# Softmax heads of 128 values: the product of the first keys' values with the probabilities in three rounded products

## Chip, cores and metric

The kernel runs on one core of one Trainium2 chip. The metric is the device time of one execution in microseconds (us). Before the change it is 1800.07 us, the median of three runs (1799.96 to 1800.71).

## The reference, cut to what matters

Four layers are applied to 256 tokens of width 2048. Each layer multiplies the normalised input with a wide weight matrix, mixes the tokens in several kinds of heads, and multiplies the result with an output matrix. All of it is in fp32. The change touches one kind of head alone, the softmax heads with 128 values:

```python
# layer 0, 8 heads (chunk_rel_attention); BAND and rel_bias give which keys count, and a bias
p = jax.nn.softmax(sc, axis=-1)
o = jnp.einsum('bhnqk,bnkhd->bnqhd', p, vb)
# layer 2, 8 heads (_dilated_mixture): causal, keys weighted by how many dilated windows hold them
# layer 3, 16 heads (_moba_attention): one block of 256 keys, so plain causal attention
s_own = jnp.where(kpos[None, :] <= qpos[:, None], s_own, -jnp.inf)
p = jax.nn.softmax(s_own, axis=-1)
return jnp.einsum('bhij,bhjd->bhid', p, vo)
```

That makes 32 such heads. Layer 2 has eight more score maps, which belong to four differential heads of 256 values; layer 1 has no softmax. The change does not touch those.

## The kernel before, in words

**The weights set the rhythm.** All weight matrices together are cut into 633 pieces of 512 KB. For each piece p, SyncE loads RAW; ScalarE rounds it to WH (the high part, type fp32r, in `split`, L1222); VectorE subtracts the two and gets WL (the low part, `split`, L1654); TensorE multiplies WH and WL with the activations, which are kept in high and low parts as well (`products`, L838 to L853). Three rounded products, high by high, low by high and high by low, stand there for one fp32 product. ScalarE and VectorE split piece p+5 in the iteration in which TensorE multiplies piece p. ScalarE may not split piece p+5 before TensorE has finished piece p-1, because there are six WH buffers.

**Everything else hangs on the pieces.** A plan, made at build time, says which small steps follow which piece. Each engine runs through the pieces in order, in one instruction stream without reordering. For piece p ScalarE and VectorE first do the `split` of piece p+5; GpSimd has no split. Then, on all three, come the steps planned half a slot before, then `evacuate` if a weight matrix block (a job) ends with piece p, then the steps planned for p. TensorE does the products and then its planned steps. In the heads plan, TensorE's order within one slot is pv, pT, scores, qkT.

**A softmax head of 128 values** (`heads_plan`) goes through these steps, one round of four pieces apart:

- `scores`: TensorE multiplies queries and keys (L960, L961) into a PSUM bank; VectorE scales and masks (L1857) and takes the row maxima (L1862, L1864); ScalarE takes the exponent with the row sum (L1382, L1384); VectorE takes the reciprocal (L1884, step `rsum`); ScalarE multiplies (L1389, L1390, step `normal`, half a slot later).
- `pT`: TensorE turns the probabilities (three 128x128 transposes, L976); ScalarE copies them out of PSUM into the slot `pt_slot` in SC (L1365).
- `pv`: TensorE multiplies the values with the turned probabilities: the first 128 keys with all 256 queries (L998, fp32) and the last 128 keys with the last 128 queries (L999, fp32). VectorE (L1901), or ScalarE for heads 24 to 31 (L1429), takes the result out.

**Where the heads run.** The 8 heads of layer 0 run beside the pieces of its z and o gates, the 8 of layer 2 and heads 32 to 39 of layer 3 beside the z blocks and the first output pieces. Heads 24 to 31, the first half of layer 3, are placed elsewhere: beside the pieces of the queries and keys of the second half (jobs q1 and k1 of layer 3, four blocks each). `pT` and `pv` of these eight stand one slot later (`late` in `heads_plan`), the two steps of one head four pieces apart. With each of the eight blocks a rope job ends: VectorE adds the two halves of the accumulator and multiplies with sine and cosine (`evacuate`, kind rope, L1721, L1727, L1729), and then GpSimd adds the two parts (`evacuate` of GpSimd, L2210). On VectorE, that rope job stands in the iteration of the block's last piece, after the split of that iteration. The iterations in which these blocks end are those one slot after `pT`.

**GpSimd's queue** holds, in order of the pieces: the rope additions (L2210), the loads of the bias of layer 0's heads with a wait for their landing (L2214, L2216), products with gates (L2193, L2238), and some additions at the end of a layer.

Of the kernel before, what the change touches and what calls it, by code (L numbers as in the profile page):

```python
# [8 lines left out]
F32 = mybir.dt.float32  # L9
F32R = mybir.dt.float32r  # L10
ALU = mybir.AluOpType
ACT = mybir.ActivationFunctionType
# [155 lines left out]
def program(nc, I, out):  # L168
    ctx = ExitStack()
    with ctx:  # L170
        def sb(name, cols, dt=F32, where=ctx):
            return where.enter_context(nc.sbuf_tensor(name, [128, cols], dt))

        def sem(name):
            return ctx.enter_context(nc.semaphore(name))
# [10 lines left out]
        SEL, _ = sb("SEL", 768, F32R), sb("Y_REST", 2 * D - 768)  # L186
# [6 lines left out]
        WH = [sb(f"WH{i}", 1024, F32R) for i in range(NHL)]  # L193
        SC = sb("SC", 4096)
        C = sb("C", CW)
        ZC = sb("ZC", 1024)
        S5 = sb("S5", 2048)
        S6 = sb("S6", 2048)
        S0 = sb("S0", 2048)
# [24 lines left out]
        def tok(i):  # L224
            return two(S[i][:, :])
# [43 lines left out]

        def qk_slot(g):  # L270
            return SC[:, 512 * (g % 3):512 * (g % 3) + 512]

        def sc_slot(g):
            return SC[:, 1536 + 384 * (g % 3):1920 + 384 * (g % 3)]

        def pt_slot(g):
            return SC[:, 2688 + 384 * (g % 3):3072 + 384 * (g % 3)]
# [101 lines left out]
        def at_A(*key):  # L379
            return A_AT[J_OF[key]]  # L380
# [11 lines left out]
        def head_of(a):  # L392
            return (0, 0, a) if a < 8 else (2 + (a - 8) // 16, (a - 8) // 8 % 2, a % 8)
# [14 lines left out]

        TURN = list(accumulate(0 if g >= 4 and first_of_pair(g - 4) else 1 for g in range(44)))

        def masked(a):

            return 2 * a + 2 if a < 8 else a + 9
# [9 lines left out]
        def put(slot, step, item=0, wants=0):  # L423
            plan.setdefault(slot, []).append((step, item, wants))
# [23 lines left out]
        def heads_plan(first, slot, every):  # L448
            for r in range(11):
                for i, step in ((3, "pv"), (2, "pT"), (1, "scores"), (0, "qkT")):  # L450
                    if step == "qkT" and first >= 8:
                        continue
                    h = r - i + (first >= 8)
                    if 0 <= h < 8:
                        late = 1 if first == 24 and step[0] == "p" else 0
                        put(slot + every * r + late, step, first + h + (4 if step[0] == "p" else 0), 1)
                        if step == "scores":
                            put(slot + every * r, "rsum", first + h)
                            put(slot + every * r + 0.5, "normal", first + h)
# [155 lines left out]
        def around(p):  # L615
# [13 lines left out]
        s_hi, s_lo, s_mm, s_evA, s_evD = (sem(n) for n in ("s_hi", "s_lo", "s_mm", "s_evA", "s_evD"))  # L629
# [8 lines left out]
        s_qkT, s_qk, s_sc, s_msk, s_mx, s_rc, s_mix, s_mixA, s_ex, s_pt, s_pts, s_pv, s_ho = (  # L638
            sem(n) for n in ("s_qkT", "s_qk", "s_sc", "s_msk", "s_mx", "s_rc", "s_mix", "s_mixA", "s_ex", "s_pt", "s_pts", "s_pv", "s_ho"))
# [5 lines left out]
            sem(n) for n in ("s_one", "s_sel", "s_dgz", "s_dgh", "s_dgl", "s_dgt", "s_mdh", "s_mdl", "s_mdt", "s_zc"))  # L645
        s_dg, s_pa, s_pe, s_pk, s_pc, s_pm, s_zero, s_am, s_tri, s_la = (
            sem(n) for n in ("s_dg", "s_pa", "s_pe", "s_pk", "s_pc", "s_pm", "s_zero", "s_am", "s_tri", "s_la"))
        s_neg = sem("s_neg")
        s_lx, s_lc, s_ly, s_ld, s_so, s_sd, s_sa, s_or, s_on, s_gd1 = (
            sem(n) for n in ("s_lx", "s_lc", "s_ly", "s_ld", "s_so", "s_sd", "s_sa", "s_or", "s_on", "s_gd1"))  # L650
        s_lg, s_li, s_lxg, s_le, s_lq, s_ls, s_zs, s_zg, s_zh, s_zl = (
# [127 lines left out]
        def tensor(e):  # L779
# [200 lines left out]
            def values_of(g):  # L980

                if g < 4:
                    return [tok(2)[:, t, 256 * g:256 * g + 256] for t in range(2)], 256, (0, "vb", (0, 1, 2, 2)[g])
                layer, n, h = head_of(g - 4)
                if is_diff(g - 4):
                    c = slice(256 * (h // 2), 256 * (h // 2) + 256)
                    return [tok(2)[:, t, c] for t in range(2)], 256, (2, "v0", h // 4)
                c = slice(128 * h, 128 * h + 128)
                return [tok(3 * n + 2 if layer else 5)[:, t, c] for t in range(2)], 128, (layer, f"v{n}" if layer else "va", h // 4)

            def pv(g, b):
                v, dv, job = values_of(g)
                e.wait_ge(s_pts, TURN[g])
                e.wait_ge(s_evA, at_A(*job))
                e.wait_ge(s_evD, at_D(*job))
                o, p = bank(b), pt_slot(g)
                if dv == 128:
                    e.matmul(o[:, 0:256], v[0], p[:, 0:256], start=True, stop=False, skip_group_check=True)  # L998
                    e.matmul(o[:, 128:256], v[1], p[:, 256:384], start=False, stop=True, skip_group_check=True).then_inc(s_pv)  # L999
                    read_out[b] = finished(g - 4)  # L1000
                    return
                e.matmul(o[:, 0:dv], p[:, 0:128], v[0], start=True, stop=True)
                e.matmul(o[:, dv:2 * dv], p[:, 128:256], v[0], start=True, stop=False)
                e.matmul(o[:, dv:2 * dv], p[:, 256:384], v[1], start=False, stop=True).then_inc(s_pv)
                read_out[b] = (s_mo, 2 * g + 2) if g < 4 else finished(g - 4)
# [195 lines left out]
        def scalar(e):  # L1201
# [161 lines left out]
            def pT(g, b):  # L1363
                e.wait_ge(s_pt, TURN[g])
                e.activation(pt_slot(g), PM[b][:, 0:384], ACT.Copy).then_inc(s_pts)  # L1365

            def norm_qk(_, b):
                for j in range(2):
                    e.wait_ge(s_qsq, 16 * j + 16)
                    e.activation(ssA[j], ssA[j], ACT.Sqrt, bias=vec("eps"), scale=1.0 / 128).then_inc(s_nq)  # L1370
# [202 lines left out]
            def gate_c(item, _):  # L1573
                b, i = item
                z = ZC[:, 512 * i:512 * i + 512]
                e.wait_ge(s_evD, at_D(1, "zc", b) - 1 + i)
# [12 lines left out]
            def subln(part, _):  # L1589
                if part == 0:  # L1590
# [1 line left out]
                    e.activation(ss, ss, ACT.Sqrt, bias=vec("eps"), scale=1.0 / 256).then_inc(s_sln)  # L1592

            steps = {"seed": seed, "warm": warm, "xt": xt, "squares": squares, "root": root, "rms_a": rms_a, "gates1": gates1, "selectors": selectors, "decay_cols": decay_cols,
                     "decay_rows": decay_rows, "cols": columns_step, "rows": rows, "decay": decay, "pT": pT,
                     "norm_qk": norm_qk, "qkT": qkT, "scores": scores, "normal": normal, "silu_z": silu_z, "yT": yT, "mix1": mix1, "pv": pv, "ty": ty, "copied": copied, "silu": silu, "decays1": decays1,
                     "decays2": decays2, "norm_sq": norm_sq, "norm_sum": norm_sum, "turn_v": turn_v, "delta_a": delta_a, "tri": tri, "small_x": small_x,
                     "spread_t": spread_t, "level_x": level_x, "level_y": level_y,
# [20 lines left out]
            for t in range(2):  # L1619
                c = slice(1536, 2048)  # L1620
# [558 lines left out]
        def gpsimd(e):  # L2179
# [50 lines left out]
            def scores(a, b):  # L2230
                if a < 6:
                    e.wait_ge(s_msk, 2 * a + 2)
                    load_bias(a + 2)

            def gate_z(i, _):
                e.wait_ge(s_zT, ZT.index(J_OF[3, "zg", i]) + 1)
                e.wait_ge(*finished(24 + 2 * i + 1))
                e.tensor_tensor(y_pair(4 + i), y_pair(4 + i), z_of(J_OF[3, "zg", i]), ALU.mult).then_inc(s_gz)  # L2238
# [41 lines left out]
            def gained(b, _):  # L2280
# [3 lines left out]
                for t in range(2):  # L2284
                    e.wait_ge(s_evD, at_D(3, "out", b) - 1 + t)
                    e.tensor_tensor(Y3[:, t, c], X3[:, t, c], S0[:, c], ALU.mult).then_inc(s_gn)

            steps = {"norm_qk": norm_qk, "scale_k": scale_k, "scores": scores, "gate_z": gate_z, "cols": columns_step, "tri": tri, "gate_w": gate_w,
                     "gate_lru": gate_lru, "gate_c": gate_c, "load_mask": load_mask, "load_gain": load_gain, "gained": gained}

            def go(todo):
# [84 lines left out]
```

## Time and profile before

| what | value |
|---|---|
| median of 3 runs | 1800.07 us |
| the profiled execution | 1799.72 us |
| its span, first to last instruction | 1797.8 us |
| TensorE, products busy | 1788.5 us, 99% |
| TensorE, weight loads busy | 1622.1 us, 90% |
| VectorE busy | 1243.6 us, 69% |
| ScalarE busy | 1037.5 us, 58% |
| GpSimd busy | 154.5 us, 9% |
| mean granted TensorE clock | 0.999 |

How to read it: PE is TensorE's products, PEld its weight loads, DVE is VectorE, ACT is ScalarE, POOL is GpSimd. A product that streams many columns overlaps the end of the one before it, so TensorE's spacing is read from start to start and not from the duration of one. An fp32 product appears as two instructions of each kind in the trace. Where rows join several instructions ("x2"), the time is from the first start to the last end. The time outside the span is 1.9 us.

### The profile page before, as it was taken

To read this page: it belongs to the slowest core of one execution; us is meant where nothing else is said; L and a number is where in the kernel's file an instruction comes from. 1 tells how busy PE (TensorE), PEld (TensorE's weight loads), DVE (VectorE), ACT (ScalarE), POOL (GpSimd) and SP (SyncE) were. 2 spreads that over 40 slices of the span, in tenths; PEclk is the share of its full clock that TensorE was granted. 3 is DMA by queue.
4 is the path that set the end of the run, shared out by engine and by line. 5 is a ranking of instruction groups with operands and counts; after the bars stand their busy time and mean duration, and the time that the engine had idled before them with its cause. 6 is when DMAs were issued, how large, how long until landed. Compare 5 with 4: busy or idle time off the path is not lost.

```text
span 1797.8 us, 27226 instructions
## 1 busy us (share of the span) xinstructions
PE 1788.5 (99%) x10842; PEld 1622.1 (90%) x10842; DVE 1243.6 (69%) x1711; ACT 1037.5 (58%) x1638; POOL 154.5 (9%) x116
## 2 busy tenths in 40 slices
PE   9999999999999999999999999999999999999998
PEld 8999889888899999998889999898888999989987
DVE  6665656665666897687658888776565888767764
ACT  7435546774557765875554345576454444457853
POOL 0000000110011111100001211000000111100110
PEclk9999999999999999999999999999999999999999
DMA  9557555555555555445566655555555655555564
GB/s 370 200 171 225 182 182 190 181 175 195 190 189 167 171 171 175 154 165 169 194 207 202 199 188 176 193 180 172 190 193 196 201 199 181 174 192 183 168 220 140
DMA packets 95901, 340.30 MB, mean 189 GB/s; under 512 B 10800, under 2 KB 11184, under 8 KB 95648
## 3 DMA queue, kind: packets, MB, share of 16 engines
q1 hardware_dynamic: 94400, 334.44, 55.9%
q0 software_dynamic: 944, 3.61, 0.6%
q8 instruction: 86, 1.41, 0.3%
q10 hardware_dynamic: 432, 0.53, 0.1%
q14 instruction: 39, 0.32, 0.1%
HBM read 336.44 MB, written 2.10 MB: 188 GB/s over the span
## 4 chain that ended last, share of the span: by engine, by line
PE 99%; DMA 0%; DVE 0%; issue 0%; ACT 0%; DVEq 0%
PE ACC L838 15%; PE ACC L840 15%; PE ACC L839 15%; PE ACC L846 12%; PE ACC L843 12%; PE ACC L845 6%; PE ACC L844 6%; PE ACC L851 2%; PE ACC L852 2%; PE ACC L853 2%; PE PM L961 1%; PE PM L998 1%; PE PM L976 1%; PE PM L890 1%; PE PM L960 0%; PE PM L999 0%
## 5 line engine op out<-in xcount | busy, mean ns | idle before, releaser
L1654 DVE TENSOR_TENSOR WL<-RAW,WH 128x1024 fp32r<-128x1024 f32 (+2 forms) x631 | 793.4, 1272 | 421.8 <-ACT WH L1222 420.3
L1222 ACT ACTIVATE WH<-RAW 128x1024 fp32r<-128x1024 f32 (+2 forms) x632 | 646.9, 1038 | 382.5 <-PE ACC L840 190.2
L843 PE MATMUL ACC<-XHL,WH 128*128 128x512 f32 x1024 | 395.6, 386 | 0.0
L846 PE MATMUL ACC<-XHL,WH 128*128 128x512 f32 x1024 | 391.2, 382 | 0.0
L838 PE MATMUL ACC<-WH,XHL 128*128 128x512 f32 (+1 forms) x788 | 296.5, 376 | 0.0
L840 PE MATMUL ACC<-WH,XHL 128*128 128x512 f32 (+1 forms) x788 | 291.9, 370 | 0.0
L839 PE MATMUL ACC<-WL,XHL 128*128 128x512 f32 (+1 forms) x788 | 291.9, 370 | 0.0
L845 PE MATMUL ACC<-XHL,WL 128*128 128x256 f32 x1024 | 281.6, 275 | 0.0
L844 PE MATMUL ACC<-XHL,WL 128*128 128x256 f32 x1024 | 279.1, 273 | 0.0
L845 PEld LDWEIGHTS ACC<-XHL,WL 128*128 128x128 f32 x1024 | 193.5, 189 | 27.4
L844 PEld LDWEIGHTS ACC<-XHL,WL 128*128 128x128 f32 x1024 | 193.6, 189 | 26.5
L843 PEld LDWEIGHTS ACC<-XHL,WH 128*128 128x128 f32 x1024 | 196.5, 192 | 1.3
L846 PEld LDWEIGHTS ACC<-XHL,WH 128*128 128x128 f32 x1024 | 196.6, 192 | 0.0
L840 PEld LDWEIGHTS ACC<-WH,XHL 128*128 128x128 f32 x788 | 148.9, 189 | 18.5
L838 PEld LDWEIGHTS ACC<-WH,XHL 128*128 128x128 f32 x788 | 149.0, 189 | 18.0 <-DVE WL L1654 0.2
L839 PEld LDWEIGHTS ACC<-WL,XHL 128*128 128x128 f32 x788 | 149.0, 189 | 17.8
L2210 POOL TENSOR_TENSOR S<-S 128x512 f32<-128x512 f32 x32 | 66.5, 2078 | 479.3 <-DVE S L1729 479.3
L851 PE MATMUL ACC<-XHL,WH 128*128 128x256 f32 x384 | 106.7, 278 | 0.0
L852 PE MATMUL ACC<-XHL,WH 128*128 128x256 f32 x384 | 105.6, 275 | 0.6 <-issue 0.6
L853 PE MATMUL ACC<-XHL,WL 128*128 128x256 f32 x384 | 105.6, 275 | 0.0
L838 PE MATMUL ACC<-WH,YHB 128*128 128x512 f32 x256 | 98.1, 383 | 0.0
L839 PE MATMUL ACC<-WL,YHB 128*128 128x512 f32 x256 | 97.0, 379 | 0.0
(406 smaller groups left out, 2344.0 us busy)
## 6 DMA issues: line engine op xcount, KB each, us to landing
RAW<-in_w SPq DMA_DIRECT2D x607, 512.0 KB, 3.3
RAW<-in_wv SPq DMA_DIRECT2D x24, 344.0 KB, 3.2
X<-in_x SPq DMA_DIRECT2D x4, 512.0 KB, 11.9
Y<-in_xT SPq DMA_DIRECT2D x3, 512.0 KB, 10.6
out<-Y SPq DMA_DIRECT2D x6, 256.0 KB, 3.6
S<-in_bias POOLq DMA_DIRECT2D x8, 128.0 KB, 2.3
S<-in_od_gate_w POOLq DMA_DIRECT2D x1, 1024.0 KB, 7.1
S<-in_final_norm POOLq DMA_DIRECT2D x1, 1024.0 KB, 6.3
```

The costliest lines, as they stand in the source:

```text
L838: e.matmul(o, th, wh, start=f, stop=False, skip_group_check=seeded)
L839: e.matmul(o, th, wl, start=False, stop=False, skip_group_check=seeded)
L840: m = e.matmul(o, tl, wh, start=False, stop=l, skip_group_check=seeded)
L843: e.matmul(acc[0], wh0, pairs, start=f, stop=False, skip_group_check=True)
L844: e.matmul(acc[0][:, 0:256], wl0, pairs[:, 0], start=False, stop=l, skip_group_check=True)
L845: e.matmul(acc[1][:, 0:256], wl1, pairs[:, 0], start=f, stop=False, skip_group_check=True)
L846: m = e.matmul(acc[1], wh1, pairs, start=False, stop=l, skip_group_check=True)
L851: e.matmul(o, wh, pairs[:, 0], start=f and g % 2 == 0, stop=False, skip_group_check=True)
L852: e.matmul(o, wh, pairs[:, 1], start=False, stop=False, skip_group_check=True)
L853: m = e.matmul(o, wl, pairs[:, 0], start=False, stop=l, skip_group_check=True)
L1222: e.activation(hi, src, ACT.Copy).then_inc(s_hi)
L1654: e.tensor_tensor(lo, src, hi.bitcast(F32), ALU.subtract).then_inc(s_lo)
```

## The change

A tile PVH of 1024 columns of type fp32r is laid over ZC, which layer 1 alone uses. For each of the 32 heads a step `pv_split` is planned one slot after `pT`. In it ScalarE rounds the head's values of the first 128 keys (128x128) and the first 256 columns of the turned probabilities (128x256) into PVH, and GpSimd subtracts and leaves the low parts in PVH. PVH has one set of halves, so ScalarE waits for the `pv` of the head before. In `pv`, TensorE waits for GpSimd's second subtraction and then does three fp32r products of 256 columns in place of the fp32 product of L998. The product of the last 128 keys (L999) stays in fp32. GpSimd's `pv_split` stands in its `steps`, which run after `evacuate` of the same iteration.

```diff
-        ZC = sb("ZC", 1024)
+        with ExitStack() as first:
+            ZC = sb("ZC", 1024, F32, first)
+        PVH = sb("PVH", 1024, F32R)
...
+        def pv_halves():
+
+            return [PVH[:, x:y] for x, y in ((0, 256), (256, 512), (512, 640), (640, 768))]
...
+        def values_at(g):
+
+            layer, n, h = head_of(g - 4)
+            c = slice(128 * h, 128 * h + 128)
+            return [tok(3 * n + 2 if layer else 5)[:, t, c] for t in range(2)], (layer, f"v{n}" if layer else "va", h // 4)
+
+        def split_heads(g):
+
+            return g - 4 if g < 12 else g - 12
...
                         put(slot + every * r + late, step, first + h + (4 if step[0] == "p" else 0), 1)
+                        if step == "pT":
+                            put(slot + every * r + late + 1, "pv_split", first + h + 4)
...
# TensorE, pv
                 if dv == 128:
-                    e.matmul(o[:, 0:256], v[0], p[:, 0:256], start=True, stop=False, skip_group_check=True)
+                    ph, pl, vh, vl = pv_halves()
+                    e.wait_ge(s_pvl, 2 * split_heads(g) + 2)
+                    e.matmul(o[:, 0:256], vh, ph, start=True, stop=False, skip_group_check=True)
+                    e.matmul(o[:, 0:256], vl, ph, start=False, stop=False, skip_group_check=True)
+                    e.matmul(o[:, 0:256], vh, pl, start=False, stop=False, skip_group_check=True)
                     e.matmul(o[:, 128:256], v[1], p[:, 256:384], start=False, stop=True, skip_group_check=True).then_inc(s_pv)
...
# ScalarE
+            def pv_split(g, _):
+                v, job = values_at(g)
+                ph, _, vh, _ = pv_halves()
+                if g > 4:
+                    e.wait_ge(s_pv, TURN[g] - 1)
+                e.wait_ge(s_evA, at_A(*job))
+                e.activation(vh, v[0], ACT.Copy).then_inc(s_pvh)
+                e.wait_ge(s_pts, TURN[g])
+                e.activation(ph, pt_slot(g)[:, 0:256], ACT.Copy).then_inc(s_pvh)
...
# GpSimd
+            def pv_split(g, _):
+                v, _ = values_at(g)
+                ph, pl, vh, vl = pv_halves()
+                e.wait_ge(s_pvh, 2 * split_heads(g) + 1)
+                e.tensor_tensor(vl, v[0], vh.bitcast(F32), ALU.subtract).then_inc(s_pvl)
+                e.wait_ge(s_pvh, 2 * split_heads(g) + 2)
+                e.tensor_tensor(pl, pt_slot(g)[:, 0:256], ph.bitcast(F32), ALU.subtract).then_inc(s_pvl)
```

## Rows read from the trace of the kernel before

**Rows 1.** The page's chain that ended last, by engine, as shares of the span.

```profile
PE 99%; DMA 0%; DVE 0%; issue 0%; ACT 0%; DVEq 0%
```

**Rows 2.** TensorE's longest wait of all: total us, times, longest us.

```profile
PE PM L882 <- DVE S L1732: 1.5, 1, 1.5
```

**Rows 3.** Line L998: duration min/median/max in ns, first and last start, form.

```profile
L998 PE MATMUL PM<-SC,S x64: 379/379/379, 327.9 to 1723.0; 128*128 128x256 f32 x64
```

**Rows 4.** Timeline of TensorE, first `pv` of layer 3: start, duration, instruction.

```profile
1503.68 0.59 PE L998 MATMUL PM<-SC,S 128*128 128x256 f32 x2
1504.11 0.39 PE L999 MATMUL PM<-SC,S 128*128 128x128 f32 x2
```

**Rows 5.** Timeline of TensorE, fp32r products of 256 columns: two of them.

```profile
545.49 0.28 PE L851 MATMUL ACC<-XHL,WH 128*128 128x256 f32 x1
...
548.84 0.28 PE L851 MATMUL ACC<-XHL,WH 128*128 128x256 f32 x1
```

**Rows 6.** Groups of ScalarE's instructions by form: busy us, mean ns, idle before.

```profile
L1244 ACT ACTIVATE S<-S 128x128 f32<-128x128 f32 x32 | 9.9, 310 | 11.3 <-DVE S L1696 10.2
L1222 ACT ACTIVATE WH<-RAW 128x256 fp32r<-128x256 f32 x1 | 0.4, 401 | 0.0
```

**Rows 7.** Lines of GpSimd: duration min/median/max in ns, first and last start, form.

```profile
L2262 POOL TENSOR_TENSOR S<-S x8: 727/733/1490, 739.5 to 749.7; 128x256 f32<-128x256 f32 x8
L2210 POOL TENSOR_TENSOR S<-S x32: 1275/2192/2197, 955.6 to 1580.3; 128x512 f32<-128x512 f32 x32
```

**Rows 8.** Timeline of DVE, ACT and POOL, one round of layer 3's first heads.

```profile
1501.49 3.44 DVE L1654 TENSOR_TENSOR WL<-RAW,WH 128x1024 fp32r<-128x1024 f32 x2
1501.66 2.19 POOL L2210 TENSOR_TENSOR S<-S 128x512 f32<-128x512 f32 x1 [10.65 <-DVE S L1729]
1504.86 0.54 DVE L1857 SCALAR_TENSOR_TENSOR SC<-PM,C 128x384 f32<-128x384 f32 x1
1505.83 0.40 ACT L1382 ACTIVATE SC<-SC,SM 128x128 f32<-128x128 f32 x1 [6.72 <-DVE SM L1862]
...
1508.36 0.36 ACT L1429 ACTIVATE Y<-PM 128x256 f32<-128x256 f32 x1
...
1510.07 1.22 DVE L1654 TENSOR_TENSOR WL<-RAW,WH 128x1024 fp32r<-128x1024 f32 x1 [1.05 <-ACT WH L1222]
...
1514.61 3.42 DVE L1654 TENSOR_TENSOR WL<-RAW,WH 128x1024 fp32r<-128x1024 f32 x2
```

**Rows 9.** Timeline, last rope job of layer 3 and the `pv` due then.

```profile
1575.64 0.59 PE L998 MATMUL PM<-SC,S 128*128 128x256 f32 x2
...
1580.16 1.22 DVE L1654 TENSOR_TENSOR WL<-RAW,WH 128x1024 fp32r<-128x1024 f32 x1
...
1580.32 2.19 POOL L2210 TENSOR_TENSOR S<-S 128x512 f32<-128x512 f32 x1 [10.91 <-DVE S L1729]
1581.30 2.30 DVE L1654 TENSOR_TENSOR WL<-RAW,WH 128x1024 fp32r<-128x1024 f32 x1
```

**Rows 10.** Timeline, layer 1: a GpSimd product between two splits of VectorE.

```profile
648.49 1.95 DVE L1654 TENSOR_TENSOR WL<-RAW,WH 128x1024 fp32r<-128x1024 f32 x1
649.32 2.26 POOL L2205 TENSOR_TENSOR S<-S,C 128x512 f32<-128x512 f32 x1
...
650.37 2.29 DVE L1654 TENSOR_TENSOR WL<-RAW,WH 128x1024 fp32r<-128x1024 f32 x1
```

**Rows 11.** Timeline, layer 1: a GpSimd product beside VectorE's reads of PSUM.

```profile
600.98 1.28 POOL L2205 TENSOR_TENSOR S<-S,C 128x512 f32<-128x512 f32 x1
...
601.23 0.28 DVE L1998 TENSOR_TENSOR SC<-PM,C 128x128 f32<-128x128 f32 x1
```

**Rows 12.** Timeline of ACT and PE, a round of layer 0's heads.

```profile
333.62 0.50 ACT L1390 ACTIVATE SC<-SC,SM 128x256 f32<-128x256 f32 x1
...
340.32 0.59 PE L998 MATMUL PM<-SC,S 128*128 128x256 f32 x2
```

**Rows 13.** Busy us of each engine, granted clock and DMA, heads 24 to 31.

```profile
1478.00:1590.00 112.00, 112.00 (x663) 102.22 (x662) 89.97 (x103) 55.13 (x102) 18.05 (x9) 1.00 0.54 179
```

More of the change, by code:

```diff
@@ L647, in program @@
             sem(n) for n in ("s_dg", "s_pa", "s_pe", "s_pk", "s_pc", "s_pm", "s_zero", "s_am", "s_tri", "s_la"))
-        s_neg = sem("s_neg")
+        s_neg, s_pvh, s_pvl = sem("s_neg"), sem("s_pvh"), sem("s_pvl")
         s_lx, s_lc, s_ly, s_ld, s_so, s_sd, s_sa, s_or, s_on, s_gd1 = (
@@ L987, in values_of @@
                     return [tok(2)[:, t, c] for t in range(2)], 256, (2, "v0", h // 4)
-                c = slice(128 * h, 128 * h + 128)
-                return [tok(3 * n + 2 if layer else 5)[:, t, c] for t in range(2)], 128, (layer, f"v{n}" if layer else "va", h // 4)
+                v, job = values_at(g)
+                return v, 128, job
             def pv(g, b):
@@ L1365, in pT @@
                 e.activation(pt_slot(g), PM[b][:, 0:384], ACT.Copy).then_inc(s_pts)
+            def pv_split(g, _):
+                v, job = values_at(g)
+                ph, _, vh, _ = pv_halves()
[5 more added lines that the diff above has]
+                e.activation(ph, pt_slot(g)[:, 0:256], ACT.Copy).then_inc(s_pvh)
             def norm_qk(_, b):
@@ L1594, in scalar @@
             steps = {"seed": seed, "warm": warm, "xt": xt, "squares": squares, "root": root, "rms_a": rms_a, "gates1": gates1, "selectors": selectors, "decay_cols": decay_cols,
-                     "decay_rows": decay_rows, "cols": columns_step, "rows": rows, "decay": decay, "pT": pT,
+                     "decay_rows": decay_rows, "cols": columns_step, "rows": rows, "decay": decay, "pT": pT, "pv_split": pv_split,
                      "norm_qk": norm_qk, "qkT": qkT, "scores": scores, "normal": normal, "silu_z": silu_z, "yT": yT, "mix1": mix1, "pv": pv, "ty": ty, "copied": copied, "silu": silu, "decays1": decays1,
@@ L2286, in gained @@
                     e.tensor_tensor(Y3[:, t, c], X3[:, t, c], S0[:, c], ALU.mult).then_inc(s_gn)
-            steps = {"norm_qk": norm_qk, "scale_k": scale_k, "scores": scores, "gate_z": gate_z, "cols": columns_step, "tri": tri, "gate_w": gate_w,
+            steps = {"norm_qk": norm_qk, "scale_k": scale_k, "scores": scores, "pv_split": pv_split, "gate_z": gate_z, "cols": columns_step, "tri": tri, "gate_w": gate_w,
                      "gate_lru": gate_lru, "gate_c": gate_c, "load_mask": load_mask, "load_gain": load_gain, "gained": gained}
```

## The prediction

> **What bounds the kernel now.** I read the chain of waits first: TensorE holds 99% of it [rows 1]. The list of TensorE's waits then says whether anything holds it up: the longest wait is 1.5 us and comes at the start [rows 2]. So TensorE is the bound from end to end; work on the other engines costs nothing until TensorE waits for it, and every us that TensorE saves or loses moves the end. A sum over TensorE's instructions is therefore half of the question. The other half is whether the new operands are there when TensorE comes to them, and for that I read the timelines round by round. Averages mislead here: in the stretch of heads 24 to 31 VectorE is busy 90.0 of 112 us, ScalarE 55.1 and GpSimd 18.1 [rows 13], and yet, below, that is the place that decides.
>
> **TensorE's own part.** The fp32 product (two instructions a head, 64 in all [rows 3], so 32 heads) runs from 1503.68 to the start of its successor at 1504.11 [rows 4]: 0.43 us. The new products are of the form of the layer-1 ones, fp32r, 256 columns, a weight load for each. Between the two rows shown there are 30 of them from start to start [rows 5]: 3.35 / 30 = 0.112 us, three make 0.335. A head saves 0.095, 32 heads 3.04 us. Bounds: the rows round to 0.01 us, which is 0.3 us over 32 heads, so 2.7 to 3.4; a stall of a weight load between the two types is in no row, and the fp32 pair that follows shows none after fp32r products before.
>
> The Trainium skill, "FP8 and Floating Point Precision", section TensorE Precision Notes, counts four passes for a true fp32 product. By that rule a pass is 0.43 / 4 = 0.107, three products save one pass, and 32 heads would save 3.4 us; the rows give 0.112 for a product with its own weight load, and the sum keeps those.
>
> **ScalarE's part.** The nearest rows are 0.31 us for 128x128 and 0.40 for 128x256 [rows 6], 0.71 a head and 23 us in all. In heads 24 to 31 it comes behind the splits that ScalarE does before it stands idle for 6.72 us, waiting for VectorE's maxima [rows 8]; it is hidden there. Without that cover it would delay the exponent by 0.71 a round. Its new wait, for the `pv` of the head before, is met already, since its copy of `pT` waited for a later TensorE step. If it weren't, the splits of the weights would queue behind it.
>
> **GpSimd's part.** The nearest rows are 0.73 for 128x256 undisturbed and 1.28 for 128x512 [rows 7]; on the line through both, 128x128 is 0.45. So 1.18 us a head, 38 us in all, on an engine that is nearly idle. What counts is its place in the queue. In heads 24 to 31 the subtractions stand behind the rope addition of the same iteration, and the addition waits for VectorE's rope job. TensorE needs the result three pieces later.
>
> **VectorE is late there already, and nobody waited for it.** VectorE's round, from the end of one rope job to that of the next, is read from the pair of splits that follows each: 1501.49 [rows 8] to 1580.16 [rows 9] in six rounds, 13.11 us each. TensorE's round, from `pv` to `pv`, is 1503.68 [rows 4] to 1575.64 [rows 9] in six: 11.99. VectorE's loop has its own chain (maxima, exponent, ScalarE's split and copies, where it waits 1.05 us [rows 8], then the split, the rope job), so it falls behind by about 1.1 us a round and uses up the five pieces of lead that the weights have. It just suffices: TensorE never waits in this stage. The new wait changes which lead counts. `pv` at 1575.64 will need a subtraction that stands behind a rope job ended at 1580.16: even with subtractions that cost nothing, TensorE would stand there for 4.5 us.
>
> **The sum, on the old clock.** The first of these heads: the rope addition ends at 1501.66 + 2.19 = 1503.85 [rows 8]. The addition takes 2.19 where it takes 1.28 alone [rows 7], because it waits for VectorE's split to end, and the second split takes 2.30 instead of 1.22 because it then waits for the addition [rows 9]: the two take turns, and whoever waits goes next. In layer 1 a GpSimd product behind another one lets the split of 648.49 go first, ends at 651.58, 1.14 after that split's end at 650.44 (0.14 less than alone), and the next split in turn ends at 652.66, 1.08 after it [rows 10]. So the first subtraction waits until the second split ends, 1501.49 + 3.44 = 1504.93, takes 0.45 - 0.14 = 0.31, and the second 0.73 behind it, until 1505.97. Both are free of VectorE, which is at the masking then [rows 8], an instruction that reads PSUM; such ones run at 0.28 beside a GpSimd product that takes its normal 1.28 [rows 11]. TensorE comes at 1503.68: it waits 2.3 us. Five more heads add VectorE's lag, 1.1 each. At the seventh and last with a rope job in front, VectorE goes on with splits, without masking between: the second split ends at 1583.60 [rows 9], first subtraction 1583.91, third split 1584.99, second subtraction 0.73 - 0.14 later, 1585.58. TensorE would come at 1575.64, less the six savings of 0.095 since the first of these heads: 1575.07. All waits of the stage together are 10.5 us. The eighth head has no rope job in front and is in time.
>
> I looked for what the waits set off. Behind the waiting `pv` queue on TensorE its own `pT` and all further pieces; ScalarE's copies of both wait for them. ScalarE comes to those copies at 1508.36 [rows 8], and the `pv` released at 1505.97 is through by 1506.5, so VectorE's loop isn't slowed. Weights are ahead of TensorE all the more. The other 24 heads: in layer 0 ScalarE's normalising ends at 334.12 and TensorE's next `pv` starts at 340.32 [rows 12]; 0.71 on ScalarE and 1.18 on GpSimd, with a turn for one split (1.08), end by 337.1. The rope additions lie between 955.6 and 1580.3 [rows 7], so none is in the queue of heads 32 to 39; layer 2's softmax heads have theirs behind them as well.
>
> Net: 10.5 - 3.0 = 7.5 us longer. On the profiled execution (1799.72: its span of 1797.8 and 1.9 around it) that is 1807.2; the median of the runs is 0.35 above that execution, so I predict **1807.6**.
>
> **Bounds of the waits.** Least: no turn is lost to splits in the last round, 1582.51 + 0.45 + 0.73 = 1583.7, waits of 8.6, time 1805.7. Most: the first subtraction loses a turn to a third split as well (1.08 more) and ScalarE's 0.71 shows once, 12.3, time 1809.4. I take the middle, nearest to the turns of rows 10.
>
> The Trainium skill, "SBUF — State Buffer", section Who interferes with whom, says that a VectorE instruction with two inputs in SBUF and a GpSimd instruction that reads SBUF exclude each other, for a whole instruction. The trace agrees (2.19 and 2.30 against 1.28 and 1.22 above). By it the last subtraction ends at 1585.6; were the two merely to share, it would be the 1583.7 of the lower bound.
>
> **Rivals.**
> *Covered after all* (0.12). The subtractions arrive in time and only TensorE's saving shows: 1800.07 - 3.0 = 1797.0. For it: GpSimd is busy 9% and the `pv` is three pieces behind. Against: the order in the queue, and 1580.16 against 1575.64. It decides from the point where GpSimd is through by 1503.68 in the first round.
> *GpSimd holds up VectorE* (0.08). Each subtraction takes a turn from VectorE's loop, and its rounds get longer, not only TensorE's. For it: the 2.30 split. Against: the masking reads PSUM. At 0.3 in each of six rounds 1.8 more, 1809.4; at both subtractions' whole turns, 0.9, 5.4 more, 1813.0.
> *TensorE's clock* (0.04). The mean granted clock is 1.00 in this stage, the upper level, with no idle time before [rows 13]. Waits of 2 to 3 us are new, and if the grant falls to 1.2 GHz after the last of them, a piece of 2.6 us (a quarter of TensorE's round, less its head steps) takes 2.6 more: 1810.2. In the rounds before it, the next wait would swallow that.
> The Trainium skill, "TensorE: Matmul & The Clock Gate", section Why this matters for your kernels, warns of such gaps in a stream of products; no row here shows a fall after one.
>
> **How the numbers follow.** Forecast 0.76, own range 1805.7 to 1809.4. From 1804.0 to 1811.0 I leave out the first rival and the far end of the second and third. A measurement of this kernel tells 0.2%, 3.6 us, from no change: slower means above 1803.7. The forecast and the last two rivals lie there, 0.88. The covered case is 0.17% faster, so 0.08 of its 0.12 goes to no change and 0.04 to faster.
>
> **What would show it.** In the changed profile, TensorE's waits should list `pv` waiting for GpSimd's PVH seven times, about 2.3, five times 1.1, and 2.9 at the last, 10 to 11 us in all, between 1500 and 1590, and none for the other 25 heads. The three products should start 0.11 apart. GpSimd's subtractions should directly follow the rope addition in those seven, VectorE's rounds there should stay at 13.1, and ScalarE should be busy some 23 us more. I am wrong if TensorE waits elsewhere, if it doesn't wait, or if VectorE's round changes.

## The result, and the profile after

The changed kernel takes 1807.93 us (median of 6 runs, 1807.16 to 1811.07); the kernel before took 1800.43 us (6 runs, 1799.96 to 1801.66, three of them those of the table before). The ratio is 1.0044, with an interval of 1.0031 to 1.0057: slower by 0.44%, clear of noise. The forecast was 1807.6, its own range 1805.7 to 1809.4.

The profiled execution took 1811.07 us, at the upper end of its runs. A second profiled execution of the same kernel took 1807.63, and sums are made against that one. Of the 3.4 us between the two, 1.7 arose at the start and 1.7 behind the last wait, both with products at half the rate (told at the end). One execution in the experiments, of the reordered kernel without heads 29 and 30, fell in a slow state at 6973.81 us and is left out of its median and ratio.

The page after, busy time by engine: against the page before, GpSimd has 51.2 us more and ScalarE 15.9; none of it is on the path but the subtractions of the seven heads below.

```profile
PE 1790.9 (99%) x10874; PEld 1623.7 (90%) x10874; DVE 1244.5 (69%) x1711; ACT 1053.4 (58%) x1702; POOL 205.7 (11%) x180
```

TensorE's waits after (us in total, times, longest), which answer to [rows 2]. The first row is new: the first of the three products waits for GpSimd's second subtraction seven times. The second row is the 1.5 us at the start that was there before.

```profile
PE PM L1018 <- POOL PVH L2273: 8.9, 7, 2.6
PE PM L900 <- DVE S L1764: 1.5, 1, 1.5
```

Timeline after, the first of the heads of layer 3 and the last with a rope job in front (answering to [rows 4, 8 and 9]). The rope addition L2242 and the two subtractions L2271, L2273 follow each other on GpSimd; the first product L1018 starts when the second subtraction is through, and TensorE is idle for 2.23 and 2.56 us before it. In the last rows the second product starts 0.19 behind the first, and the pair behind the three 0.43.

```profile
1501.68 3.44 DVE L1686 TENSOR_TENSOR WL<-RAW,WH 128x1024 fp32r<-128x1024 f32 x2
1501.85 2.19 POOL L2242 TENSOR_TENSOR S<-S 128x512 f32<-128x512 f32 x1 [10.65 <-DVE S L1761]
1504.00 1.43 POOL L2271 TENSOR_TENSOR PVH<-S,PVH 128x128 fp32r<-128x128 f32 x1
1505.40 0.72 POOL L2273 TENSOR_TENSOR PVH<-SC,PVH 128x256 fp32r<-128x256 f32 x1
1506.26 0.36 PE L1018 MATMUL PM<-PVH 128*128 128x256 f32 x1 [2.23 <-POOL PVH L2273]
...
1580.32 4.83 DVE L1686 TENSOR_TENSOR WL<-RAW,WH 128x1024 fp32r<-128x1024 f32 x3
1580.48 2.19 POOL L2242 TENSOR_TENSOR S<-S 128x512 f32<-128x512 f32 x1 [8.84 <-DVE S L1761]
1582.63 1.43 POOL L2271 TENSOR_TENSOR PVH<-S,PVH 128x128 fp32r<-128x128 f32 x1
1584.03 1.70 POOL L2273 TENSOR_TENSOR PVH<-SC,PVH 128x256 fp32r<-128x256 f32 x1
1585.87 0.35 PE L1018 MATMUL PM<-PVH 128*128 128x256 f32 x1 [2.56 <-POOL PVH L2273]
1586.06 0.28 PE L1019 MATMUL PM<-PVH 128*128 128x256 f32 x1
...
1586.30 0.38 PE L1021 MATMUL PM<-SC,S 128*128 128x128 f32 x2
```

VectorE's pairs of splits that follow the rope jobs start at 1501.68 and 1580.32, six rounds apart: 13.11 us each, as in [rows 8 and 9]. VectorE's loop didn't change; TensorE's was stretched to it.

The undisturbed heads, after (the timeline of TensorE in one head of the last eight; it answers to [rows 4 and 5]): the three products start 0.116, 0.116 and 0.118 apart in the trace's ns, and the pair behind them 0.35 after the first, where the successor of the fp32 product stood 0.43 after it. Over the 25 heads that don't wait it's 0.350 to 0.361, 0.356 in the mean: 0.119 a product.

```profile
1662.67 0.28 PE L1018 MATMUL PM<-PVH 128*128 128x256 f32 x1
1662.79 0.28 PE L1019 MATMUL PM<-PVH 128*128 128x256 f32 x1
1662.91 0.28 PE L1020 MATMUL PM<-PVH 128*128 128x256 f32 x1
1663.02 0.39 PE L1021 MATMUL PM<-SC,S 128*128 128x128 f32 x2
```

**Where the time went.** The start of the `pv` of a head, before and in the second execution after, gives the sum (us from the span's start, from both traces):

| head | before | after | difference | what lies between |
|---|---|---|---|---|
| 0 | 327.89 | 328.43 | +0.54 | the start of the program, other than between two executions |
| 7 | 414.29 | 414.30 | +0.01 | seven heads, 0.075 saved each |
| 16 | 1190.09 | 1189.29 | -0.80 | one head, and 0.74 at 780.8 that nobody had forecast |
| 23 | 1275.35 | 1274.01 | -1.34 | seven heads, 0.075 each |
| 30 | 1575.64 | 1584.30 | +8.66 | the seven waits, less head 23's saving: 10.0 |
| 39 | 1722.77 | 1730.82 | +8.05 | 0.61 in the eight heads that don't wait |

The end is 7.91 us later than in the profiled execution before (1799.72). In it are the waits (+10.1, counted by the starts), the saving of the 25 heads that don't wait (-1.9), a stall that went away (-0.74), and the start (+0.5). The heads have the numbers of the code; 8 to 15 are not softmax heads of 128 values. The list of waits has 9.0 for the same seven (2.23, five times 0.83 to 0.84, 2.56), not 10.1: it counts idle time from the end of the product before, and in a stream a product starts some 0.16 ahead of that end (0.28 long, 0.12 apart in the rows above), so each wait shifts a start by some 0.16 more than the list shows.

### The profile page after: what moved, and what is told of

The parts are those of the page before. It is cut to its first block, busy times and chain, and to the rows that moved or that the text cites. A ratio compares the mean times of both kernels' runs of the same rounds, so it can differ in the third digit from the quotient of the medians.

```text
span 1809.1 us, 27449 instructions
## 1 busy us (share of the span) xinstructions
PE 1790.9 (99%) x10874; PEld 1623.7 (90%) x10874; DVE 1244.5 (69%) x1711; ACT 1053.4 (58%) x1702; POOL 205.7 (11%) x180
## 4 chain that ended last, share of the span: by engine, by line
PE 93%; DVE 4%; ACT 2%; DMA 1%; issue 0%; POOL 0%; DVEq 0%; ACTq 0%
PE ACC L856 15%; PE ACC L858 15%; PE ACC L857 15%; PE ACC L864 11%; PE ACC L861 11%; PE ACC L863 6%; PE ACC L862 5%; PE ACC L869 2%; PE ACC L870 2%; PE ACC L871 2%; DVE WL L1686 2%; PE PM L979 1%; DVE S L1759 1%; ACT WH L1244 1%; PE PM L994 1%; PE PM L908 1%
## 5 line engine op out<-in xcount | busy, mean ns | idle before, releaser
L2242 POOL TENSOR_TENSOR S<-S 128x512 f32<-128x512 f32 x32 | 66.4, 2076 | 461.3 <-DVE S L1761 461.3
L858 PE MATMUL ACC<-WH,YLB 128*128 128x512 f32 x256 | 97.0, 379 | 0.0
```

The costliest lines, as they stand in the source:

```text
L858: m = e.matmul(o, tl, wh, start=False, stop=l, skip_group_check=seeded)
```

## The experiments

In all of these the kernel before ran beside them on the same chip: 1800.28 us (median of 21 runs) beside the first four, 1800.08 (17 runs) beside the others.

**Only GpSimd's queue reordered.** The subtractions of heads 24 to 31 are put half a slot earlier, ahead of the rope addition of the same iteration; TensorE's, VectorE's and ScalarE's instructions keep their order.

```diff
-                            put(slot + every * r + late + 1, "pv_split", first + h + 4)
+                            put(slot + every * r + late + (0.5 if first == 24 else 1), "pv_split", first + h + 4)
```

> The same instructions as in the changed kernel; only GpSimd's queue is reordered: in heads 24 to 31 the two subtractions of a head stand ahead of the rope addition of the same iteration. Theory (the 10.5 us are the place in the queue, behind an addition that waits for VectorE's late rope job): the seven waits of TensorE for the second subtraction are gone, or 0.5 us at most are left where the weights' low parts are only 0.2 us ahead; the saving of 0.075 us a head stays in all 32 heads, 2.4 us, and the time is 1800.4 - 2.4 = 1798.0 (1797.5 to 1798.8). Rival (the cost is GpSimd's work itself, its turns with VectorE, wherever it stands): VectorE's rounds become longer than 13.11 us, by up to the 1.66 us that the two subtractions take, TensorE waits for low parts of the weights in their place, and the time is 1802 or more.

Measured: 1799.84 us (median of 11), ratio 1.0000, interval 0.9991 to 1.0009. Five of the seven waits are gone, but two are left, at heads 29 and 30, and the time is 1.8 above the expectation. First its list of TensorE's waits, then its timeline around the last.

```profile
PE PM L1018 <- POOL PVH L2273: 2.4, 2, 1.6
```

```profile
1560.20 0.30 ACT L1395 ACTIVATE PVH<-S 128x128 fp32r<-128x128 f32 x1
...
1569.21 0.40 ACT L1414 ACTIVATE SC<-SC,SM 128x128 f32<-128x128 f32 x1 [6.51 <-DVE SM L1894]
...
1572.00 0.47 ACT L1387 ACTIVATE SC<-PM 128x384 f32<-128x384 f32 x1
1572.37 1.05 ACT L1244 ACTIVATE WH<-RAW 128x1024 fp32r<-128x1024 f32 x1
1573.32 0.30 ACT L1395 ACTIVATE PVH<-S 128x128 fp32r<-128x128 f32 x1
...
1573.69 1.30 POOL L2271 TENSOR_TENSOR PVH<-S,PVH 128x128 fp32r<-128x128 f32 x1 [6.46 <-ACT PVH L1395]
1574.95 0.73 POOL L2273 TENSOR_TENSOR PVH<-SC,PVH 128x256 fp32r<-128x256 f32 x1
1575.83 0.35 PE L1018 MATMUL PM<-PVH 128*128 128x256 f32 x1 [1.58 <-POOL PVH L2273]
```

What follows: the place in the queue was most of the price (from head 23 to head 30 this kernel falls back 2.3 us against the one before, and the changed kernel 10.0), but my theory stopped one step short. GpSimd now waits 6.46 us for ScalarE's rounding copy, and that copy (1560.20, then 1573.32) has VectorE's round of 13.12 as well, because it stands in ScalarE's queue behind the exponent, which waits for VectorE's maxima (1569.21), and ScalarE isn't idle between the two. So the low parts still fall behind TensorE's 12.04 by 1.08 us a head; from their new place they merely start with more lead, which lasts for five heads. The rival is out: VectorE's rope products L1761 start at 1498.68 in the first of these rounds and at 1577.38 in the last, 13.12 a round.

**The subtractions on VectorE.** In heads 24 to 31 VectorE does them right behind its rope job; GpSimd's step returns there.

```diff
...
+            def pv_split(g, _):        # VectorE
+                if not 28 <= g < 36:
+                    return
+                v, _ = values_at(g)
+                ph, pl, vh, vl = pv_halves()
+                e.wait_ge(s_pvh, 2 * split_heads(g) + 1)
+                e.tensor_tensor(vl, v[0], vh.bitcast(F32), ALU.subtract).then_inc(s_pvl)
+                e.wait_ge(s_pvh, 2 * split_heads(g) + 2)
+                e.tensor_tensor(pl, pt_slot(g)[:, 0:256], ph.bitcast(F32), ALU.subtract).then_inc(s_pvl)
...
```

> In heads 24 to 31 the two subtractions are done by VectorE, right behind its rope job, and not by GpSimd; the other 24 heads as in the changed kernel. Theory (VectorE's rope job is late, whoever stands behind it): VectorE's round grows from 13.11 us by about 0.5, TensorE waits for VectorE now, first some 0.5 us at the first of these heads instead of 2.2 and then 1.6 a round; the last product would start near 1580.40 + 6 x 0.54 + 0.54 = 1584.2, where it started at 1585.87: about 1806.2 (1805 to 1808). Rival (GpSimd is too slow or too far for this work): without GpSimd the waits are gone, 1798 to 1799.

Measured: 1807.96 us (median of 5; the profiled execution 1806.46), ratio 1.0041, interval 1.0028 to 1.0053: inside the range of the theory. Its TensorE waits, and its timeline at the last:

```profile
PE PM L1018 <- DVE PVH L1943: 8.8, 6, 2.1
```

```profile
1580.70 0.69 DVE L1761 TENSOR_TENSOR S<-S,C 128x512 f32<-128x512 f32 x1
1581.31 0.28 DVE L1941 TENSOR_TENSOR PVH<-S,PVH 128x128 fp32r<-128x128 f32 x1
1581.47 1.26 POOL L2252 TENSOR_TENSOR S<-S 128x512 f32<-128x512 f32 x1 [12.39 <-DVE S L1761]
1581.52 1.50 DVE L1943 TENSOR_TENSOR PVH<-SC,PVH 128x256 fp32r<-128x256 f32 x1
```

What follows: taking GpSimd out doesn't help, so GpSimd's speed is not the cause. Whoever stands behind the rope job is late. VectorE's round grew to 13.66 (its rope products start at 1498.75 and 1580.70, six apart), 0.55 a round as expected. The sizes inside were not quite as expected: no wait at the first of the heads, 1.14 at the second, 1.4 at the next four and 2.12 at the last, where the second subtraction takes 1.50, as the rope addition, released by the same rope job, starts ahead of it and ends at 1582.73, 0.29 before it.

**The wait without the saving.** All copies, subtractions and waits stay; TensorE does the fp32 product of before in place of the three, and the high and low parts are not used.

```diff
-                    e.matmul(o[:, 0:256], vh, ph, start=True, stop=False, skip_group_check=True)
-                    e.matmul(o[:, 0:256], vl, ph, start=False, stop=False, skip_group_check=True)
-                    e.matmul(o[:, 0:256], vh, pl, start=False, stop=False, skip_group_check=True)
+                    e.matmul(o[:, 0:256], v[0], p[:, 0:256], start=True, stop=False, skip_group_check=True)
```

> All copies, subtractions and waits of the changed kernel, but TensorE does the fp32 product of before in place of the three, so the high and low parts are computed and waited for and not used. Theory (the wait and the saving are two terms that add up): the waits cost 10.0 + 7 x 0.075 less nothing: TensorE comes later by the saving it no longer has, so the waits sum to 10.0 and the time is 1800.4 + 10.0 = 1810.4 (1809.5 to 1812.2 with the clock's dip after the last wait, 1.7 us). Rival (part of the 7.5 us is that the three products are slower than thought, or that their neighbours are): 1807 or less.

Measured: 1811.95 us (median of 5, 1810.21 to 1812.39), ratio 1.0062, interval 1.0049 to 1.0076: inside the range of the theory. Its list of TensorE's waits:

```profile
PE PM L1018 <- POOL PVH L2271: 7.5, 6, 2.5
PE PM L900 <- DVE S L1762: 1.5, 1, 1.5
PE ACC L870 <- issue: 0.7, 1, 0.7
```

What follows: waits and saving add up as two terms. The profiled execution (1812.2) is 12.5 above the one of before: 1.9 from its start, 10.2 from the waits by the starts, 0.4 because the clock fell after the first wait and VectorE's next round was 13.53 instead of 13.11. The list has six waits and not seven: behind that fall TensorE came late enough at the second head to find its low parts ready. The third row was a surprise: a stall of 0.66 us in which TensorE waits for nothing that the profile shows. The kernel before has the same (timeline of TensorE before, where the 780.81 row follows one of 779.91), and the changed kernel has none.

```profile
780.81 0.27 PE L852 MATMUL ACC<-XHL,WH 128*128 128x256 f32 x1 [0.62 <-issue]
```

**Without heads 24 to 31.** These eight are done as before the change, with one fp32 product and no copies; the other 24 as changed.

```diff
...
-                        if step == "pT":
+                        if step == "pT" and first != 24:
...
+                    if 28 <= g < 36:
+                        e.matmul(o[:, 0:256], v[0], p[:, 0:256], start=True, stop=False, skip_group_check=True)
+                    else:
...
```

> Heads 24 to 31 are done as before the change (one fp32 product, no copies, no subtractions); the other 24 heads as in the changed kernel. Theory: no wait is left, 24 heads save 0.075 us each, 1800.4 - 1.8 = 1798.6 (1798.2 to 1799.2). Rival (the other 24 heads pay too, in waits or in ScalarE's copies): 1800 or more.

Measured: 1797.06 us (median of 11), ratio 0.9983, interval 0.9974 to 0.9991: faster than both kernels. No wait for the products is in its list, whose longest row is the one at the start:

```profile
PE PM L900 <- DVE S L1767: 1.5, 1, 1.5
```

What follows: the other 24 heads pay nothing. It is 1.1 us below the expected range, a miss, and the trace says why: 24 heads save 1.82, and the stall at 780.8 is gone here too, another 0.74. 1799.72 - 1.82 - 0.74 = 1797.16; the profiled execution took 1797.14.

**What a product costs.** The forecast took 0.112 us from product to product, and the trace shows more. The number and the order of a head's products are varied by groups of heads.

```diff
+                    if g < 12:
+                        e.matmul(o[:, 0:256], vh, pl, start=False, stop=False, skip_group_check=True)
+                        e.matmul(o[:, 0:256], vl, ph, start=False, stop=False, skip_group_check=True)
+                    elif g < 28:
+                        e.matmul(o[:, 0:256], vl, ph, start=False, stop=False, skip_group_check=True)
...
+                        e.matmul(o[:, 0:256], vl, pl, start=False, stop=False, skip_group_check=True)
```

> Where the 0.116 us from product to product comes from (the forecast took 0.112). The changed kernel, with the products of a head varied by group, so the output is not the reference's: heads 0 to 7 in the order vh x ph, vh x pl, vl x ph (the same stationary operand twice running); heads 16 to 23 without the third product; heads 24 to 31 as in the change; heads 32 to 39 with a fourth product, vl x pl. From the start of the first product to the start of the instruction pair behind them: theory (each product costs 0.116 to 0.117, whatever its neighbours): 0.350, 0.233, 0.350, 0.467. Rival 1 (a fixed extra of some 0.014 once a head, at the change from the fp32 type to fp32r and back, and 0.112 for a product): 0.350, 0.238, 0.350, 0.462. Rival 2 (the change of the stationary operand costs it): heads 0 to 7 are shorter than heads 24 to 31.

Measured (one execution, 1809.52 us): from the first product to the pair behind, in the mean of the eight heads, 0.358 for the other order (0.358 in the changed kernel's own order, same heads), 0.240 for two products, 0.475 for four. Timeline of TensorE, one head of each group; the last row of each is the pair.

```profile
390.13 0.28 PE L1018 MATMUL PM<-PVH 128*128 128x256 f32 x1
...
390.49 0.38 PE L1031 MATMUL PM<-SC,S 128*128 128x128 f32 x2
...
1249.27 0.28 PE L1018 MATMUL PM<-PVH 128*128 128x256 f32 x1
1249.38 0.28 PE L1023 MATMUL PM<-PVH 128*128 128x256 f32 x1
1249.50 0.39 PE L1031 MATMUL PM<-SC,S 128*128 128x128 f32 x2
...
1684.78 0.28 PE L1018 MATMUL PM<-PVH 128*128 128x256 f32 x1
...
1685.26 0.38 PE L1031 MATMUL PM<-SC,S 128*128 128x128 f32 x2
```

What follows: two, three and four products cost 0.119 to 0.120 each, a little more than the theory's 0.116 to 0.117. A line through the three means rises by 0.118 a product and leaves 0.004 for a fixed price, so rival 1 (0.112 and 0.014) is out. The order doesn't matter, against rival 2; but the trace has a weight load ahead of every product, also where the operand stays the same, so what the load itself costs is not shown. Why 256 columns out of PVH take 0.119 where those of layer 1 took 0.112 stays open.

**Reordered, and without heads 29 and 30.** The first experiment's queue, with fp32 products in the two heads whose low parts were late.

```diff
...
-                        if step == "pT":
+                        if step == "pT" and first + h not in (29, 30):
...
-                            put(slot + every * r + late + 1, "pv_split", first + h + 4)
+                            put(slot + every * r + late + (0.5 if first == 24 else 1), "pv_split", first + h + 4)
...
+                    if 33 <= g < 35:
+                        e.matmul(o[:, 0:256], v[0], p[:, 0:256], start=True, stop=False, skip_group_check=True)
+                    else:
...
```

> The reordered GpSimd queue of the run before_rope, with the two heads that still waited there (29 and 30) done as before the change: one fp32 product, no copies, no subtractions. Theory: ScalarE's rounding copies follow VectorE's rounds of 13.11 us, so the high and low parts lose 1.07 us a head against TensorE and come in time for heads 24 to 28 and 31 only; with 29 and 30 on the fp32 product no wait of TensorE is left (0.3 us at most, for the weights' low parts, which have 0.2 us to spare at the last round and lose 0.075 for each head that is shorter). 30 heads save 0.0755 us each, 2.27, and the stall of 0.6 to 0.8 us at 780.8 stays away as in the other kernels with more TensorE instructions: 1799.7 - 2.27 - 0.75 = 1796.7 where the clock rises early at the start, 1798.7 where it rises late; median 1796.7 (1796.2 to 1797.6). Rival (the two rounds without the copies change ScalarE's and VectorE's loop, or the low parts of the weights are now late): 1798 or more with a wait of 0.5 us or more in the stage of heads 24 to 31.

Measured: 1797.29 us (median of 11), ratio 0.9985, interval 0.9976 to 0.9993: inside the range of the theory, faster than both kernels, not told apart from the 24 heads by its time. Its list of TensorE's waits has no row between 1480 and 1600; behind the 1.5 us at the start the longest is

```profile
PE PM L933 <- DVE S L1827: 1.0, 1, 1.0
```

What follows: the account by lead holds, head by head. Between head 0 and head 39 this kernel gains 2.8 us on the one before, the kernel with 24 heads 2.5. In the profiled execution that row, a wait that ends at 175.47 and is up to 0.3 us long in the others, took it back.

**Layer 0 as before.** The changed kernel with fp32 products in heads 0 to 7 alone.

```diff
...
-                        if step == "pT":
+                        if step == "pT" and first > 0:
...
+                    if g < 12:
+                        e.matmul(o[:, 0:256], v[0], p[:, 0:256], start=True, stop=False, skip_group_check=True)
+                    else:
...
```

> The changed kernel with the eight heads of layer 0 done as before the change, so that TensorE's instructions up to 780 us are those of the kernel before. The stall of 0.6 us at 780.81, in which TensorE waited for nothing that the profile shows, was there in the kernel before and in the run with the fp32 product in all heads, and in no kernel with the three products in layer 0. Theory (what TensorE has run up to that point places it): it is back, 0.6 to 0.7 us at the same instruction. Rival (the length of the whole program or its memory layout decides, or it comes by chance): no such stall there. Waits of the heads 24 to 31 as in the changed kernel, 8.9 us by the list of waits.

Measured (one execution, 1810.28 us): the seven waits as expected, and the stall is back at the same instruction of the same stretch, at 780.99, though shorter: 0.35 where the theory said 0.6 to 0.7. Its list of TensorE's waits, then its timeline of TensorE there:

```profile
PE PM L1021 <- POOL PVH L2276: 8.9, 7, 2.5
...
PE ACC L870 <- issue: 0.4, 1, 0.4
```

```profile
780.37 0.28 PE L869 MATMUL ACC<-XHL,WH 128*128 128x256 f32 x1
780.99 0.27 PE L870 MATMUL ACC<-XHL,WH 128*128 128x256 f32 x1 [0.35 <-issue]
```

What follows: it goes with TensorE's instructions up to that point. The three kernels that run fp32 products in layer 0 have it, one of them with all copies and subtractions of the change, and the six others don't. What it is, no row shows.

**The changed kernel again, for the clock.**

> The changed kernel once more, for the clock. Theory: the seven waits before the first product are the same within 0.1 us (2.2, 0.8 five times, 2.6), since VectorE sets them; the fall of the granted clock behind a wait of over 2 us is not tied to it, so it can stand behind the first wait, the last or none, and the time is 1807.0 without a fall that counts, 1808.7 with one behind the last wait, each 2.0 more where the clock rises late at the start. Rival (the fall follows from the wait of 2.56 us itself): it is behind the last wait again.

Measured (one execution): 1807.63 us, without a fall and 0.6 above the expectation for that; the seven waits 2.23, 0.83 to 0.84 five times, and 2.56, as expected. The first fence is its row of TensorE's waits; the second its stretch behind the last wait, the third the same stretch in the first profiled execution (busy time of PE, PEld, DVE, ACT and POOL, then the granted clock, DMA share and GB/s).

```profile
PE PM L1018 <- POOL PVH L2273: 9.0, 7, 2.6
```

```profile
1588.00:1590.00 2.00, 2.00 (x11) 1.76 (x10) 0.95 (x2) 1.06 (x1) 1.18 (x2) 1.00 0.40 102
```

```profile
1588.00:1590.00 2.00, 2.00 (x7) 1.55 (x6) 1.23 (x1) 0.99 (x3) 1.24 (x1) 0.50 0.04 8
```

What follows: the same wait of 2.56, once with the clock at 1.00 behind it and once at 0.50. So the wait alone doesn't set the fall; the rival is out.

## Why the prediction came out right, and where it didn't

**The waits: right in place and number, in size by the starts alone.** In the last round the first subtraction was to end at 1583.91 and the second at 1585.58 on the old clock. VectorE's last splits start 0.16 later in the execution after (1580.32 for 1580.16), so 1584.07 and 1585.74; they end at 1584.06 and 1585.73. The stretch from head 23 to head 30 costs 10.0 us; the forecast had 9.8 there, 10.5 of waits less the savings. But the prediction also wanted 10 to 11 us in the list of waits, 2.3, five times 1.1 and 2.9, and the list has 9.0, with 2.23, five times 0.83 and 2.56. It had worked out shifts of starts and looked for them in a list of idle times. By the starts the seven are 2.4, five times 1.0 and 2.7.

The ends of the first subtractions are in part luck. The prediction let one take 0.31 behind VectorE's split, as 0.45 alone less 0.14; alone it takes 0.61 (the median of all 32), and behind the split it again took 0.31 (1505.12 to 1505.43 in the first round). Two errors cancel.

The Trainium skill, "SBUF — State Buffer", section Who interferes with whom, was the rule behind the turns: a VectorE instruction with two inputs in SBUF and a GpSimd instruction that reads SBUF exclude each other for a whole instruction. The runs agree: 1.43 and 1.70 us for subtractions beside VectorE's splits, 0.61 and 0.73 in the median of all 32.

**The saving: right in kind, too large.** The term 0.43 - 0.335 = 0.095 a head measured 0.431 - 0.356 = 0.075, because a product takes 0.119 and not 0.112. And a head that has waited saves nothing against the kernel before: its second product starts 0.193 after the first, so the three take 0.43, like the fp32 pair without a wait. It's the wait that costs this, not the type: in the run that keeps the fp32 product it takes 0.507 behind a wait (1588.11 to 1588.62 at the last of them), 0.075 more than the 0.432 it takes without one. 25 heads save 1.9 us; the forecast had 2.4 for them, and 0.7 for the seven others.

The Trainium skill, "FP8 and Floating Point Precision", section TensorE Precision Notes, counts four passes for an fp32 product. An estimate from that count would make three products save a quarter, 0.108 a head. No run here shows that saving: it's 0.075 a head, and the measurement decides.

**What was missing.** The stall at 780.8, 0.74 us in the change's favour. Set out in the same parts, the forecast was 10.5 less seven heads' 0.67, 9.8, for the heads that wait, and -2.4 for the other 25; measured are 10.1, -1.9 and -0.74. Both sum to some 7.5. So the waits cost 0.3 more and the saving is 0.5 less than forecast, the stall makes up for both, and the closeness of 1807.6 to 1807.93 is partly luck. The six runs spread from 1807.16 to 1811.07, and only the profiled one's clock can be followed in time; how far falls of the clock moved their median is not known.

**Covered work: right.** ScalarE's copies cost nothing: 15.9 us more busy and not 23, since they overlap. GpSimd's 128x128 takes 0.61 alone, not the 0.45 of my line, and its 51 us for 38 show nowhere outside those seven heads. The 24 heads of the fourth experiment show the same from the other side.

**The rivals.** *Covered after all* fell with the seven waits. *GpSimd holds up VectorE* fell with 13.11 us a round. *The clock* was priced too high (2.6) and taken as another case, where it is one part of some executions: behind the last wait of over 2 us the clock fell in three of five. In the first profiled execution head 31 starts 11.92 late where head 30 started 10.23 late: 1.7 us.

**What the experiments corrected.** The reason that I gave, the place in GpSimd's queue, was true for what the change does and incomplete as a cure. Beneath it lies a lead that VectorE's round of 13.11 eats up against TensorE's 12.0, in everything that hangs on VectorE: the rope job first, then ScalarE's copies as well.

## What to carry to other kernels

Before new work is hung on a nearly idle engine, look at what stands ahead of it in that engine's queue, and at the round of the engine that releases it: a lead that shrinks each round decides, not busy shares. When one stage spoils a change, leave that stage out: 24 of 32 heads made 1797.1 of 1807.9. And undo the pieces one at a time even when the forecast fits; here errors of 0.8 us in all were cancelled by a stall of 0.74 that nobody had counted.

## What the runs showed of the hardware that was not expected

**TensorE's clock behind a wait.** Ten waits of 2.2 to 2.6 us stand in five profiled executions. After five of them the granted clock fell from 1.00, the level of 2.4 GHz, to 0.50, the level of 1.2 GHz, for 3.4 us, and products of 512 columns took 0.63 us instead of 0.38; after the other five it stayed at 1.00. Behind the waits of 0.5 to 1.6 us and one of 2.12 it never fell. A fall behind a wait that is followed by another was made up for in that next wait, save for 0.4 us through VectorE; the one behind the last wait cost 1.7. These are ten cases; what decides between a fall and none, no run shows.

**The first products.** Some executions start 2 us slower than others of the same kernel. In the first profiled execution of the changed kernel, products of 512 columns stand 0.43 apart up to 10 us, in the second 0.21 apart from 6 us on; the profile's clock column reads 1.00 in both. The trace's clock records, from which that column comes, begin only at 10.18 us in the first and at 5.84 in the second, both with 1.00, and the column counts the time ahead of them as 1.00. Timeline of TensorE, the first execution, then the second:

```profile
6.43 0.63 PE L847 MATMUL ACC<-WH,XHL 128*128 128x512 f32 x1
6.85 0.63 PE L846 MATMUL ACC<-WH,XHL 128*128 128x512 f32 x1
```

```profile
6.49 0.38 PE L847 MATMUL ACC<-WH,XHL 128*128 128x512 f32 x1
...
7.14 0.38 PE L846 MATMUL ACC<-WH,XHL 128*128 128x512 f32 x1
```

The runs of the kernel with 24 heads stand in two groups for it, eight at 1796.65 to 1797.63 and three at 1798.95 to 1799.09. These 2 us are more than the 1.8 us that 24 heads save: without several runs of either kernel the best version here couldn't have been told from the one before.

**A stall that comes and goes with the instruction stream.** 0.35 to 0.66 us in the gap's own row, near 781 (782.8 in the one that started late), and the profile ties it to no wait for a buffer or a queue. The Trainium skill, "Runtime: NRT & Kernel Launch", section Instruction fetch mechanics, tells of instructions being fetched in blocks while the engine runs, mostly hidden; that this is such a fetch, no run here shows.
